# One pass of squares for two norms in a row: the sums of squares move to TensorE

## The chip, the cores and the metric

The kernel runs on one NeuronCore of a Trainium2 chip. The number that counts is the device time of one execution in microseconds (us), of which the median of the runs is taken.

## The reference, cut to what matters

The reference is a transformer block of width 1024 over 512 positions, then a second model of two layers whose input is the output of the first and 256 context rows. What is computed where the change lies:

```
x = x + gate2 * ((gelu(u_gate) * u_val) @ w_down)      # end of the first block
x = rmsnorm(x, g_final)                                # its final norm ("gfinal")
# second model, layer 0:
h = rms_norm(x, norm_g) * (1 + scale) + shift          # for the 512 latent rows, and the same for the 256 context rows
proj = h @ w_in                                        # first products: "pre"
rmsnorm(x, g) = x * rsqrt(mean(x*x) + 1e-6) * g
```

So two norms stand directly behind each other. All data are float32; the wide products split each operand into a rounded high part and a low part and add three products (high*high, low*high, high*low).

## The kernel before, in words

Activations are kept transposed: `XT` holds x as eight row groups of 128 channels by 512 positions, `CT` the context as eight of 128 by 256. The program is a list of stages (`plan()`), and each engine runs the stages in order from an instruction stream that is written out by hand. Counting semaphores `S[...]` order the engines, with a base count for each stage. Behind each stage stands a fence (line 3026): the engine drains, counts up, and in most stages waits for the other engines' counts. Nothing is scheduled automatically.

Around the change the stages are `up`, `down`, `gfinal`, `layer` (the norm of layer 0) and `pre`.

- `up` (PE line 2392, ACT 2656, DVE 2873) makes 22 groups F of the gated hidden layer. A group takes two 128x1024 weight blocks. ACT rounds a block into its high part (`act_high`, line 615), DVE makes its low part (`dve_low`, line 625), PE multiplies (`pe_split`, line 651), DVE does the convolution (lines 2890 to 2894), ACT the gelu (2665), DVE the gating product (`gated`, 2878). After the last group ACT rounds F rows 0 and 1 (2670) and DVE makes their low part (2911), which PE's first block of `down` needs. DVE then writes the modulation vectors (2693, 2698).
- `down` (PE 2411, ACT 2639, DVE 2919) has 22 weight blocks of 24 matmuls. Blocks with an even number add into PSUM banks 0 to 3 and those with an odd number into banks 4 to 7. Block 20 ends the first half and block 21 the second; DVE adds each half into `XT`, four times line 2941. ACT's DMA of the context rows into `SQ_ROWS` is issued in `down` (line 2035).
- `gfinal`: ACT squares each of the eight rows of `XT` (line 2092), DVE adds them up into one row `RS` (line 2055, one addition a row, each with a drain, three of them already between the halves of `down`), PE multiplies that row with ones, which gives the sum of each position (`pe_sums`, line 2072), ACT takes the root (2100), DVE the reciprocal (2143), PE spreads it over the partitions (`pe_spread`, 2062), and DVE scales `XT` in place, eight instructions (2150). Ahead of the sums PE transposes the context rows, 16 transposes (2021), which DVE copies into `CT` (2029).
- `layer` does the same again for the scaled `XT` and for `CT` together, 768 columns. Then DVE scales each row into a buffer (2150), ACT rounds it with the shift added (2110), DVE writes the low part (2160), and counts `low_row`. ACT and DVE first split the two first weight blocks of `pre` (615, 625).
- `pre` (PE 2433, ACT 2672, DVE 2947): PE's first two weight blocks go row by row behind `low_row` (`pe_rows_two`, line 655), then four more blocks j = 2 to 5. DVE copies each product out (2958) and splits the weights ahead. PE sums squares of the results in the same way as above (`pe_latent`, line 2203), without an addition ahead: the squares of three rows are multiplied with ones one after the other.

fp32 matmuls and sums appear in the trace as two instructions for each 128x128 tile (8 for four tiles), fp32 transposes as one.

## Time and profile before

| what | value |
|---|---|
| three runs | 3863.46, 3870.72, 3872.88 us |
| median | 3870.72 us |
| profiled execution, its own time | 3862.4 us |
| span inside it | 3860.6 us |
| TensorE (PE) busy | 3640.3 us, 94% |
| VectorE (DVE) busy | 2043.3 us, 53% |
| ScalarE (ACT) busy | 1426.3 us, 37% |
| mean granted TensorE clock | 0.975 of 2.4 GHz |

Times of the trace are counted from the start of the span. A row of the timeline view gives start, length, engine, line, operation and tiles, the number of merged instructions, and in brackets the idle time of that engine before it with what ended it. `<-DVE probs L2055` means that the wait ended when DVE's instruction on line 2055 did. `PEld` is TensorE's loading of the stationary operand.

### The profile page before, as it was taken

The numbers are of one execution on the slowest core, as the hardware profiler recorded it, in microseconds if no ns is written. First come the engines' busy times: TensorE is split into PE (matmuls) and PEld (weight loads), VectorE is DVE, ScalarE is ACT, GpSimd is POOL, SyncE is SP. The second block draws the span as 40 slices with busy tenths as digits, with TensorE's granted clock in tenths as the row PEclk, the third lists the DMA queues.
The fourth block names the chain that finished last, engine by engine and source line by source line (L and its number), as shares of the span: only waits on it lengthen the run. The fifth ranks groups of instructions, "written<-read, shape, count | busy, mean of one in ns | idle before, by whom it ended". The sixth has DMA issues, their size and how long they took to land.

```text
span 3860.6 us, 54876 instructions
## 1 busy us (share of the span) xinstructions
PE 3640.3 (94%) x20163; PEld 2824.5 (73%) x20163; DVE 2043.3 (53%) x3393; ACT 1426.3 (37%) x2534; POOL 265.7 (7%) x196
## 2 busy tenths in 40 slices
PE   6998989999799999999999999998999999999998
PEld 4665768878667788777778776886668777676666
DVE  4555346553545533777733555244553567645544
ACT  3433233323333322444431545122333344524532
POOL 0000000000011001111000100000110221001100
PEclk9998989999799999999999999997999999999999
DMA  7553325543101122211112111211113222131122
GB/s 257 158 138 95 92 85 165 167 139 109 50 21 30 27 65 58 52 48 50 44 49 57 42 28 50 66 55 49 29 37 93 61 64 55 49 92 51 42 77 79
DMA packets 506585, 286.93 MB, mean 74 GB/s; under 512 B 48129, under 2 KB 485469, under 8 KB 506438
## 3 DMA queue, kind: packets, MB, share of 16 engines
q1 hardware_dynamic: 485979, 264.60, 24.6%
q10 hardware_dynamic: 20459, 20.36, 1.8%
q8 instruction: 94, 1.54, 0.2%
q14 instruction: 53, 0.43, 0.0%
HBM read 269.05 MB, written 10.32 MB: 72 GB/s over the span
## 4 chain that ended last, share of the span: by engine, by line
issue 90%; PE 3%; POOL 3%; POOLq 2%; DVE 1%; ACT 0%; DVEq 0%; ACTq 0%
PE ps L629 3%; POOLq L1385 2%; POOL qT L1384 2%; POOL qT L1386 1%; POOL y_and_merged L1384 1%; DVEq L3028 0%; DVE w_low L625 0%; PE ps L2472 0%; DVE probs L911 0%; PE ps L1070 0%; POOLq L212 0%; DVE h_low L2270 0%; DVE y_low L2803 0%; ACT w_high L615 0%; DVE y_and_merged L3005 0%
## 5 line engine op out<-in xcount | busy, mean ns | idle before, releaser
L629 PE MATMUL ps<-h_high,w_high 128*128 128x512 f32 (+1 forms) x3432 | 1285.0, 374 | 45.9 <-DVE w_low L625 24.5
L629 PE MATMUL ps<-h_low,w_high 128*128 128x512 f32 (+1 forms) x3432 | 1246.7, 363 | 0.0
L629 PE MATMUL ps<-h_high,w_low 128*128 128x512 f32 (+1 forms) x3432 | 1243.7, 362 | 0.0
L629 PEld LDWEIGHTS ps<-h_high,w_high 128*128 128x128 f32 x3432 | 652.7, 190 | 209.5 <-issue 60.5
L625 DVE TENSOR_TENSOR w_low<-w_raw,w_high 128x1024 fp32r<-128x1024 f32 x374 | 463.3, 1239 | 590.2 <-ACT w_high L615 568.0
L629 PEld LDWEIGHTS ps<-h_high,w_low 128*128 128x128 f32 x3432 | 652.7, 190 | 103.3
L629 PEld LDWEIGHTS ps<-h_low,w_high 128*128 128x128 f32 x3432 | 654.0, 191 | 93.7 <-issue 3.1
L615 ACT ACTIVATE w_high<-w_raw 128x1024 fp32r<-128x1024 f32 x374 | 387.8, 1038 | 641.1 <-PE ps L629 549.4
L890 ACT ACTIVATE probs<-ps,neg_max 128x768 f32<-128x768 f32 (+1 forms) x240 | 194.8, 815 | 407.0 <-DVE neg_max L922 406.8
L629 PE MATMUL ps<-probsT,v 128*128 128x512 f32 (+4 forms) x736 | 285.7, 557 | 14.0 <-DVE probsT L1133 8.7
L922 DVE TENSOR_REDUCE neg_max<-ps 128x1 f32<-128x768 f32 (+1 forms) x240 | 196.7, 847 | 162.9 <-PE ps L629 152.9
L629 PE MATMUL ps<-y_high,w_high 128*128 128x512 f32 (+1 forms) x640 | 230.4, 360 | 8.1 <-issue 6.5
L629 PE MATMUL ps<-k_high,q_high 64*128 64x256 f32 (+4 forms) x784 | 181.5, 385 | 57.1 <-DVE neg_max L908 19.2
L629 PE MATMUL ps<-y_high,w_low 128*128 128x512 f32 (+1 forms) x640 | 229.8, 359 | 0.0
L890 ACT ACTIVATE probs<-probs,neg_max 128x512 f32<-128x512 f32 (+1 forms) x192 | 145.6, 758 | 172.0 <-DVE neg_max L914 123.1
L629 PE MATMUL ps<-y_low,w_high 128*128 128x512 f32 (+1 forms) x544 | 194.9, 358 | 0.0
L629 PEld LDWEIGHTS ps<-k_high,q_high 64*128 64x128 f32 (+1 forms) x784 | 88.9, 186 | 128.8 <-issue 31.5
L1019 PEld LDWEIGHTS ps<-ident,probs 128*128 128x128 f32 x832 | 101.6, 141 | 94.8 <-issue 85.3
L629 PE MATMUL ps<-k_low,q_high 64*128 64x256 f32 (+4 forms) x784 | 153.1, 323 | 0.0
L629 PE MATMUL ps<-k_high,q_low 64*128 64x256 f32 (+4 forms) x784 | 152.8, 322 | 0.0
L2807 DVE SCALAR_TENSOR_TENSOR probs<-probs,ps 128x512 f32<-128x512 f32 x88 | 51.9, 613 | 189.6 <-PE ps L629 189.6
L1133 DVE COPY probsT<-ps 128x512 f32<-128x512 f32 x112 | 73.2, 654 | 142.8 <-PE ps L1019 142.3
(250 smaller groups left out, 4158.6 us busy)
## 6 DMA issues: line engine op xcount, KB each, us to landing
w_raw<-in_w_in SPq DMA_DIRECT2D x436, 256.0 KB, 3.2
y_and_merged<-in_w_mod SPq DMA_DIRECT2D x96, 256.0 KB, 3.2
w_raw<-in_w_branch SPq DMA_DIRECT2D x96, 256.0 KB, 3.0
w_raw<-in_w_up SPq DMA_DIRECT2D x88, 256.0 KB, 4.3
y_and_merged<-in_w_ada SPq DMA_DIRECT2D x64, 256.0 KB, 3.2
w_raw<-in_w_out SPq DMA_DIRECT2D x48, 256.0 KB, 3.0
w_raw<-in_w_down SPq DMA_DIRECT2D x44, 256.0 KB, 3.2
y_and_merged<-in_w_ada SPq DMA_DIRECT2D x4, 2048.0 KB, 17.2
```

The costliest lines, as they stand in the source:

```text
L615: act.activation(WR[:, k, 0:nk], WRAW[:, k, 0:nk], ACT.Copy).then_inc(s_high, 1)
L625: nc.vector.tensor_tensor(WL[:, k, 0:nk], WRAW[:, k, 0:nk], WR[:, k, 0:nk].bitcast(F32), ALU.subtract).then_inc(s_low, 1)
L629: return nc.tensor.matmul(*a, **kw)
L890: act.activation(it["dst"], src, ACT.Exp, bias=NM[:, idx:idx + 1], accum_out=SL[:, idx:idx + 1]).then_inc(S["exped"], 1)
L922: v.tensor_reduce(NM[:, idx:idx + 1], src, AXX, ALU.max, negate=True).then_inc(S["maxed"], 1)
L1019: last = nc.tensor.transpose(PS[:, b:b + 128], tile, ident[:, :])
L1133: nc.vector.tensor_copy(PT[:, which, 0:m], PS[:, b:b + m]).then_inc(S["pt_dve"], 1)
L1384: g.tensor_tensor(x, x, cos, ALU.mult)
L1385: g.drain()
L1386: g.tensor_tensor(x, x, swapped, ALU.add).then_inc(S["roped"], 1)
L2807: v.scalar_tensor_tensor(out=d, in0=d, scalar=1.0, in1=p, op0=ALU.add, op1=ALU.mult)
```

## The change

The `layer` norm of layer 0 no longer has squares, sums, root and reciprocal of its own. In `gfinal` ACT squares the eight rows of `XT` once, into six buffers, and PE multiplies each square row as it comes with a pair of columns: ones, and g_final squared plus epsilon (`NORM_PAIR`). The second column gives the mean from which the root of both norms together follows: ACT takes it with a bias of epsilon squared (`EPS2`), and DVE's scaling in `layer` uses `GAINS`, the product of both gains, on the unscaled `XT`. The first column gives the final norm's own root `RX`, with which DVE scales `XT` itself later, two rows behind each of j = 1 to 4 of `pre`. The context rows' sums of squares come from two squaring instructions of ACT with an accumulated output, in block pair 3 of `down`. DVE's additions of squares (42 in the kernel before, line 2055) lose those of these two norms. PE transposes twelve context tiles ahead of the sums and four behind them; DVE copies all of them after the reciprocal. The two first weight splits of `pre` move to ahead of and in between the squares (ACT) and to behind the halves of `down` (DVE). PE no longer waits at the fence behind `down`, nor DVE at that behind `gfinal`. In `up`, the rounding of F rows 0 and 1 and their low part stand ahead of the last groups in place of behind them, and DVE's end of `up` gets five small instructions and two drains for the new columns.

```diff
+def shares_sums(s):
+    return s["what"] == "layer" and s["l"] == 0
...
         if k == "norm":
-            add(s, square=s["nk"], added=s["nk"] - 1, square_mm=1, rstd=1, rinv=1, spread=1)
+            if not shares_sums(s):
+                add(s, square=s["nk"], added=s["nk"] - 1, square_mm=1, rstd=1, rinv=1, spread=1)
             if s["what"] == "gfinal":
-                add(s, fin=8)
+                add(s, rstd=1, spread=1, fin=1)
...
+        NORM_PAIR = YM[:, 16 * TOK - 256:16 * TOK - 240].rearrange("p (k e) -> p k e", e=2)
+        GAINS = YM[:, 16 * TOK - 240:16 * TOK - 232]
+        EPS2 = YM[:, 16 * TOK - 232:16 * TOK - 231]
+        RX = YM[:, 16 * TOK - 228:16 * TOK - 224]
...
-            return [(x, 0, LAT, AC[:, 2 + 2 * l, kc:kc + 1], MOD[:, b, 0:1]),
+            return [(x, 0, LAT, GAINS[:, kc:kc + 1] if l == 0 else AC[:, 4, kc:kc + 1], MOD[:, b, 0:1]),
...
+        CT_BANKS = (1, 2, 3, 6)
+        def x_squares(kc):
+            return PP[:, 512 * (kc % 6):512 * (kc % 6) + 512]
+        def pe_both_norms(pe, s):
+            def turn(j):
+                for e in range(2):
+                    for a in range(2):
+                        kc = 2 * j + e
+                        last = nc.tensor.transpose(bank(CT_BANKS[j], 128, 256 * e + 128 * a), SQ_ROWS[:, a, 128 * kc:128 * kc + 128], ident[:, :])
+                last.then_inc(S["x_t"], 1)
...
+            pe.wait_ge(S["ctx_in"], s.base["ctx_in"] + 32)
+            pe.wait_ge(S["down_ev"], s.base["down_ev"] - 4)
+            for j in range(3):
+                turn(j)
+            for kc in range(NK):
+                pe.wait_ge(S["square"], s.base["square"] + kc + 1)
+                for tt in range(4):
+                    last = mm(bank(0, 2, 2 * tt), x_squares(kc)[:, 128 * tt:128 * tt + 128], NORM_PAIR[:, kc, :], start=kc == 0 and tt == 0,
+                              stop=kc == NK - 1, skip_group_check=True)
+                last.then_inc(S["added"] if kc < NK - 1 else S["square_mm"], 1)
+            turn(3)
+            pe.wait_ge(S["rinv"], s.base["rinv"] + 1)
+            pe_spread(4, RT, True).then_inc(S["spread"], 1)
+            pe.wait_ge(S["fin"], s.base["fin"] + 1)
+            pe_spread(7, RX, False).then_inc(S["spread"], 1)
+        def act_both_norms(act, s):
+            first = Stage("first", h_end=None).at(s.base)
+            act_high(act, first, 0, 0, 0)
+            for kc in range(NK):
+                if kc == 4:
+                    act_high(act, first, 0, 0, 1)
+                act.wait_ge(S["down_ev"], s.base["down_ev"] - 8 + kc + 1)
+                if kc >= 6:
+                    act.wait_ge(S["added"], s.base["added"] + kc - 5)
+                act.activation(x_squares(kc), XT[:, kc, :], ACT.Square).then_inc(S["square"], 1)
+            act.drain()
+            act.activation(RT[:, 4:6], RT[:, 4:6], ACT.Sqrt, scale=1.0 / D, bias=EPSB[:, :])
+            act.wait_ge(S["square_mm"], s.base["square_mm"] + 1)
+            sums = bank(0, 8).rearrange("p (a e) -> p a e", e=2)
+            act.activation(RT[:, 0:4], sums[:, :, 1], ACT.Sqrt, scale=1.0 / D, bias=EPS2).then_inc(S["rstd"], 1)
+            act.activation(RX, sums[:, :, 0], ACT.Sqrt, scale=1.0 / D, bias=EPSB[:, :]).then_inc(S["rstd"], 1)
+        def dve_both_norms(dve, s):
+            def rows(j):
+                dve.wait_ge(S["x_t"], s.base["x_t"] + 8 + j + 1)
+                nc.vector.tensor_copy(CT[:, 2 * j:2 * j + 2, :], bank(CT_BANKS[j]).rearrange("p (e t) -> p e t", e=2))
+            dve_low(dve, Stage("first", h_end=None).at(s.base), 0, 0, 1)
+            dve.wait_ge(S["rstd"], s.base["rstd"] + 1)
+            nc.vector.reciprocal(RT[:, 0:6], RT[:, 0:6]).then_inc(S["rinv"], 1)
+            rows(0)
+            rows(1)
+            dve.wait_ge(S["rstd"], s.base["rstd"] + 2)
+            nc.vector.reciprocal(RX, RX)
+            rows(2)
+            rows(3)
+            nc.vector.drain().then_inc(S["fin"], 1)
+        def dve_scaled_x(s, rows):
+            for kc in rows:
+                nc.vector.scalar_tensor_tensor(out=XT[:, kc, :], in0=XT[:, kc, :], scalar=VT[:, V_GFIN + kc:V_GFIN + kc + 1], in1=bank(7),
+                                               op0=ALU.mult, op1=ALU.mult)
         def pe_norm(pe, s):
-            if s["what"] == "h1":
+            if s["what"] == "h1" or shares_sums(s):
                 return
-            if s["rows"]:
-                pe_rows(pe, s)
...
             pe_sums(pe, s)
...
+            if s["what"] == "gfinal":
+                act_both_norms(act, s)
+                return
+            if shares_sums(s):
+                for kc in range(nk):
+                    act_rounded(act, s, kc)
+                return
...
-                if s["what"] == "gfinal":
-                    act.wait_ge(S["down_ev"], s.base["down_ev"] - 8 + kc + 1)
-                if s["what"] == "layer" and s["l"] == 0:
-                    act.wait_ge(S["fin"], s.base["fin"] - 8 + kc + 1)
                 act_row(act, s, kc)
...
-            if s["what"] == "gfinal":
-                last.then_inc(S["fin"], 1)
...
-            if s["what"] == "layer" and s["l"] == 0:
-                for j in range(2):
-                    dve_low(dve, Stage("first", h_end=None).at(s.base), 0, 0, j)
-            for kc in range(6 if done_in_out(s) else 4 if s["rows"] else 1, NK):
+            if s["what"] == "gfinal":
+                dve_both_norms(dve, s)
+                return
+            if shares_sums(s):
+                dve.wait_ge(S["spread"], s.base["spread"] - 1)
+                for kc in range(NK):
+                    dve_scaled(dve, s, kc)
+                    if kc:
+                        dve_low_row(dve, s, kc - 1)
+                dve_low_row(dve, s, NK - 1)
+                return
+            for kc in range(6 if done_in_out(s) else 1, NK):
                 dve_add(dve, s, kc, s["ctx"])
-            if s["rows"]:
-                dve_rows(dve, s, (0, 1))
...
             dve_inverse(dve, s)
-            if s["rows"]:
-                dve_rows(dve, s, (2, 3))
...
+                    if kb == 3:
+                        act.wait_ge(S["ctx_in"], stages[s.index + 1].base["ctx_in"] + 32)
+                        for a in range(2):
+                            act.activation(PP[:, D * a:D * a + D], SQ_ROWS[:, a, :], ACT.Square, accum_out=RT[:, 4 + a:5 + a])
+                        act.drain()
                     for e in range(2):
                         act_high(act, s, 0, 0, 2 * kb + 2 + e)
...
                 repeat(act, NF - 2, 2, body)
-                for u in range(2):
-                    body(NF // 2 - 1, u, NF - 2 + u)
                 for a in range(2):
                     last = act.activation(f_rows(0, a)[0], F[:, a, :], ACT.Copy)
                 last.then_inc(S["f_high"], 1)
+                for u in range(2):
+                    body(NF // 2 - 1, u, NF - 2 + u)
...
                 with dve.Fori(1, NF // 2 - 1) as t:
                     for u in range(2):
                         body(t, u, t * 2 + u)
-                for u in range(2):
-                    body(NF // 2 - 1, u, NF - 2 + u)
-                gated(NF // 2 - 1, 1, NF - 1)
+                body(NF // 2 - 1, 0, NF - 2)
                 dve.wait_ge(S["f_high"], s.base["f_high"] + 1)
                 for a in range(2):
                     fh, fl = f_rows(0, a)
                     last = v.tensor_tensor(fl, F[:, a, :], fh.bitcast(F32), ALU.subtract)
                 last.then_inc(S["f_low"], 1)
+                body(NF // 2 - 1, 1, NF - 1)
+                gated(NF // 2 - 1, 1, NF - 1)
                 dve.wait_ge(S["mod_sum"], s.base["mod_sum"] + 44)
                 modulation(v, 52, 96, bank(7, 88), V_BMOD + 4)
                 v.drain()
                 for a, (m0, c, g) in enumerate(((56, 0, V_NG), (56, 1, V_NG), (80, 0, V_NG + 8), (80, 1, V_NG + 8))):
                     norm_scale(v, a + 2, m0, c, g)
+                gain = VT[:, V_GFIN:V_GFIN + 8]
+                v.memset(NORM_PAIR[:, :, 0], 1.0)
+                v.memset(EPS2, EPS * EPS)
+                v.tensor_tensor(NORM_PAIR[:, :, 1], gain, gain, ALU.mult)
+                v.drain()
+                v.tensor_scalar(NORM_PAIR[:, :, 1], NORM_PAIR[:, :, 1], EPS, None, ALU.add)
+                v.tensor_tensor(GAINS, AC[:, 2, :], gain, ALU.mult)
+                v.drain()
...
                     if hf == 0:
-                        v.drain()
-                        for kc in range(1, 4):
-                            dve_add(dve, s, kc, False)
+                        dve_low(dve, Stage("first", h_end=None).at(stages[s.index + 1].base), 0, 0, 0)
...
                     last.then_inc(S["mm_ev"], 1)
+                    if l == 0 and 1 <= j <= 4:
+                        if j == 1:
+                            dve.wait_ge(S["spread"], s.base["spread"])
+                        dve_scaled_x(s, (2 * j - 2, 2 * j - 1))
...
                 return
-            if me == "act" and (s.kind == "down" or s["what"] == "gfinal"):
+            if me in ("act", "pe") and s.kind == "down" or s["what"] == "gfinal":
                 return
-            if me == "pe" and (s["what"] == "gfinal" or s.kind == "up"):
+            if me == "pe" and s.kind == "up":
                 return
             for other in s_fence:
```

## Rows read from the trace of the kernel before

The columns of the timeline are start us, length us, engine, line, operation, out<-in, shapes and count, [idle before <- what ended it]. The columns of the stretches are length, busy us of PE, PEld, DVE, ACT and POOL (each with its count), granted clock, share of the DMA engines, GB/s.

**Rows 1.** First part of the page: busy time of each engine.

```profile
PE 3640.3 (94%) x20163; PEld 2824.5 (73%) x20163; DVE 2043.3 (53%) x3393; ACT 1426.3 (37%) x2534; POOL 265.7 (7%) x196
```

**Rows 2.** Waits of PE: engine, tile, line, releaser: total us, times, longest.

```profile
PE ps L629 <- DVE probs L2055: 27.8, 4, 15.2
```

**Rows 3.** Timeline of PE around the two norms, 978 to 1013 us.

```profile
978.01 0.39 PE L629 MATMUL ps<-h_high,w_low 128*128 128x512 f32 x1
981.31 3.32 PE L2021 MATMUL ps<-ident,probs 128*128 128x128 f32 x16 [2.91 <-DVEq L3028]
...
986.12 1.16 PE L629 MATMUL ps<-ident,rstd_rows 128*128 128x128 f32 x8 [0.57 <-DVE rstd_rows L2143]
1002.50 2.72 PE L629 MATMUL ps<-ones,probs 128*128 128x2 f32 x12 [15.22 <-DVE probs L2055]
1005.80 2.93 PE L629 MATMUL ps<-ident,rstd_rows 128*128 128x128 f32 x12 [0.58 <-DVE rstd_rows L2143]
1012.38 0.77 PE L629 MATMUL ps<-h_high,w_high 128*128 128x512 f32 x1 [3.66 <-DVE h_low L2160]
```

**Rows 4.** Timeline of DVE, same stretch.

```profile
978.43 2.73 DVE L2941 SCALAR_TENSOR_TENSOR xT<-ps,mod,xT 128x512 f32<-128x512 f32 x4 [0.28 <-PE ps L629]
...
984.54 1.29 DVE L2029 COPY y_and_merged<-ps 128x512 f32<-128x512 f32 x2
...
987.32 5.35 DVE L2150 SCALAR_TENSOR_TENSOR xT<-xT,vectors,ps 128x512 f32<-128x512 f32 x8
...
995.19 7.25 DVE L2055 TENSOR_TENSOR probs<-probs 128x768 f32<-128x768 f32 x7
...
1008.76 0.75 DVE L2150 SCALAR_TENSOR_TENSOR probs<-xT,norm_scale,ps 128x512 f32<-128x512 f32 x1 [3.02 <-PE ps L629]
```

**Rows 5.** Timeline of ACT, same stretch.

```profile
973.86 1.95 ACT L2092 ACTIVATE probs<-xT 128x512 f32<-128x512 f32 x3 [5.19 <-DVE xT L2941]
...
986.02 2.00 ACT L615 ACTIVATE w_high<-w_raw 128x1024 fp32r<-128x1024 f32 x2 [0.17 <-issue]
...
1005.25 0.27 ACT L2100 ACTIVATE rstd_rows<-ps,eps 128x6 f32<-128x6 f32 x1 [3.94 <-PE ps L629]
```

**Rows 6.** PE's thin work at the full clock, elsewhere (timeline).

```profile
1049.18 4.73 PE L629 MATMUL ps<-ones,probs 128*128 128x2 f32 x36
...
2534.64 1.96 PE L2021 MATMUL ps<-ident,probs 128*128 128x128 f32 x16
```

**Rows 7.** Busy time by stretch; the number behind POOL is the granted clock.

```profile
983.00:984.00 1.00, 1.00 (x7) 1.00 (x6) 0.91 (x2) 0.55 (x1) 0.00 (x0) 0.50 0.02 8
984.50:986.00 1.50, 1.05 (x10) 0.97 (x8) 1.40 (x4) 0.26 (x1) 0.00 (x0) 1.00 0.00 0
...
1051.00:1052.00 1.00, 1.00 (x11) 1.00 (x11) 0.00 (x0) 0.28 (x1) 0.00 (x0) 1.00 0.00 0
...
1053.00:1054.00 1.00, 1.00 (x6) 1.00 (x6) 0.00 (x0) 0.05 (x1) 0.00 (x0) 0.50 0.00 0
```

**Rows 8.** Edge from `up` to `down`: PE (timeline, then clock), DVE, ACT.

```profile
855.91 0.76 PE L629 MATMUL ps<-q_high,w_high 128*128 128x512 f32 x1 [4.34 <-DVE k_low L2911]
...
855.90:861.00 5.10, 5.09 (x12) 4.04 (x13) 2.83 (x7) 2.00 (x2) 0.00 (x0) 0.50 0.17 50
...
846.05 1.23 DVE L625 TENSOR_TENSOR w_low<-w_raw,w_high 128x1024 fp32r<-128x1024 f32 x1 [3.98 <-ACT w_high L615]
...
852.03 0.75 DVE L2894 SCALAR_TENSOR_TENSOR probs<-ps,vectors,probs 128x511 f32<-128x511 f32 x1
...
831.43 1.06 ACT L615 ACTIVATE w_high<-w_raw 128x1024 fp32r<-128x1024 f32 x1 [1.33 <-DMA w_raw<-in_w_up]
...
856.56 1.06 ACT L615 ACTIVATE w_high<-w_raw 128x1024 fp32r<-128x1024 f32 x1 [2.08 <-DVEq L3028]
```

**Rows 9.** Cover in `down` (ACT) and in `pre` (DVE), timeline.

```profile
962.17 1.06 ACT L615 ACTIVATE w_high<-w_raw 128x1024 fp32r<-128x1024 f32 x1 [3.43 <-PE ps L629]
...
1074.60 1.02 DVE L2958 COPY qT<-ps 96x512 f32<-96x512 f32 x2 [3.76 <-PE ps L629]
```

11 lines of the change are left out of this document (6 added, 5 removed).

## The prediction

> **What bounds the kernel now.** I read the page first: TensorE is busy 94% of the span, no other engine over 53% [rows 1]. So a gain must come from places where TensorE stands still or runs at half clock. Next the list of PE's waits: its largest is the one for DVE's additions of squares on line 2055, 27.8 us in four waits, one of them 15.2 us long [rows 2]. Then PE's timeline where that long wait lies. The last matmul of `down` starts at 978.01 and ends at 978.40; the first matmul of `pre` starts at 1012.38 [rows 3]. Between them PE only has 16 transposes, two small sums and two spreadings. **34.0 us** pass in which the chain over DVE and ACT sets the time: DVE brings x up to date until 981.16, adds, scales XT in place for 5.35 us, adds again for 7.25 us over 768 columns, and scales from 1008.76 [rows 4]. From that first scaling to the first matmul of `pre` it is 1012.38 - 1008.76 = 3.62 us [rows 3, 4]. Last I read the granted clock of the same stretch and of others with thin matmuls [rows 7], and the edge from `up` to `down`, which the change also touches [rows 8].
>
> **The change, part by part: between the norms.** Out of the path go the second set of squares and additions, the second root, reciprocal and spreading, and the 5.35 us of scaling XT. What is new on the path is PE's: 8 rows by 4 tiles by 2 = 64 instructions in place of 8 and 12.
>
> The start: PE no longer waits 2.91 us for the fence [rows 3]. Its twelve transposes need the context and the first half's banks, both there. They begin at about 978.45. Such a transpose took 1.96/16 = 0.123 us at the full clock [rows 6], so 1.5 us, until 979.95. Squares are ready by then: ACT splits the first weight block from about 973.1 (1.00 us each by rows 5), then squares rows 0 to 3 at 0.65 us each [rows 5] until 976.8. It takes the second block at 978.43 and rows 4 to 7 from 979.45; the last cannot begin ahead of DVE's last update, 981.16 [rows 4], and is done by about 983 with its wait for a free buffer. PE needs it only after seven rows of sums, so ACT is never last. DVE's splits (two, one in the half break and one behind 981.16) also lie ahead of what comes.
>
> The sums: 4.73/36 = 0.131 us each at the full clock [rows 6], 2.72/12 = 0.227 us at half [rows 3]. 64 cost 8.4 us or 14.5 us. Which clock? In the row with 36 such sums in one piece the clock was 1.00 at 1051 and 0.50 at 1053 [rows 7], although PE had no gap: dense thin sums did not keep the clock, and it fell some 3.3 us into them. I take the same here: it falls 3.4 us after 978.45, at 981.85. By then (981.85 - 979.95)/0.131 = 14 sums are done; 50 x 0.227 = 11.3 us follow, so the sums end at 993.2. Bounds: full clock throughout, 988.4; half clock from the first transpose, 978.45 + 12 x 0.207 [3.32/16, rows 3] + 14.5 = 995.5.
>
> Behind the sums: from their end to the first spreading it was 1005.80 - 1005.22 = 0.58 us for root and reciprocal [rows 3, 5]. Four transposes stand ahead of the spreading now, 0.83 us at half clock, so it starts 0.83 behind the sums; twelve instructions of 2.93 us [rows 3], and DVE starts 0.03 later: 3.8 us. Beside it DVE makes the reciprocal, four copies at 0.65 us [rows 4], a second reciprocal and a drain: about 0.5 + 2.6 + 0.2 + 0.2 = 3.5 us, hidden (at full clock PE needs 0.58 + 1.16 x 12/8 = 2.3 us and DVE's 3.5 us become the path). Then 3.62 us as before. First matmul of `pre`: 993.2 + 3.8 + 3.6 = 1000.6, against 1012.38: **11.8 us saved**. The bounds: 995.5 + 7.4 = 1002.9, which saves 9.4; 988.4 + 3.5 + 3.6 = 995.5, which saves 16.9. The second spreading of PE (eight, 1.16 us [rows 3] to 1.95 us) waits for DVE's `fin` and falls into the 3.66 us in which PE waits for the first `low_row` [rows 3]. I cost it at nothing; without that cover it is 2 us.
>
> Here a page speaks against the change. The clock at 983 was 0.50 and at 984.5 it was 1.00 [rows 7], with nothing but transposes in between [rows 3]. The Trainium skill, TensorE: Matmul & The Clock Gate, section Part 4: PE-mode transpose, says that transposes do not count as TensorE being busy. This trace disagrees for these fp32 transposes. By the page the twelve new ones would help the clock fall and the sum would go to its slow bound, 9.4 us; by the row they hold it for a while.
>
> **In `pre`.** XT's eight scalings, 5.35 us [rows 4], are now two behind each of four products, 1.34 us at a time. DVE waits for PE there: ahead of the last copy it still stood idle for 3.76 us [rows 9], the shortest of the stretches these fall in. Cost nothing; uncovered they would be 5.4 us. In `down` ACT gets two squares of 1024 columns, about 1.1 us each with the accumulator (estimate from its 1.06 us for 1024 columns [rows 9]), into an idle piece of 3.43 us [rows 9]. Nothing; without the cover 2.2 us. The weights' DMAs on SP's queue wait for DVE's splits, which come sooner than before.
>
> **The edge from `up` to `down`.** PE waited 4.34 us for the low part of F row 1 and began at 855.91 [rows 8]. Both roundings now stand ahead of ACT's split at 831.43, where it waited 1.33 us for a DMA, and cost about 1.2 us; both low parts stand ahead of DVE's at 846.05, with 3.98 us idle and a cost of 1.3 us [rows 8]. Hidden. What is late next is the last convolution, 852.03 + 0.75 = 852.78, for which PE waits too. So PE starts at 852.88, 3.0 us sooner. The new small instructions (about 0.8 us, an estimate: root and reciprocal of six columns took 0.58 together [rows 3], hand-overs included, for two of them) lie behind DVE's gating product, which moved up by as much as the low parts took (1.3 us). ACT's next split was at 856.56, behind DVE's fence [rows 8], and comes at about 856, so block 1 can start at 858.3, when block 0 (24 matmuls of 0.227, 5.45 us) ends. And the clock: before, the first twelve matmuls ran at 0.50 [rows 8], 0.427 in place of 0.227 us, which cost 2.4 us. With 1.3 us of idle in place of 4.3 the clock may hold or fall later. Bounds 0 and 2.4 us, less 0.2 for the wait of block 1; I take 1.4, a little over the middle, since the idle time is so much shorter. **4.4 us saved**, bounds 3.0 and 5.2.
>
> **The sum.** 11.8 + 4.4 = 16.2 us. Against the profiled execution's own time that is 3862.4 - 16.2 = 3846.2. That execution stood 8.3 us under the median of the runs shown (3870.72), within their spread of 9.4 us; on the scale of the median it is **3854.5 us**.
>
> **The rivals.**
> First, the clock holds: full speed through sums and edge, 16.9 + 5.2 = 22.1 us, 3848.6 us. For it, the clock stood at 1.00 in the sums of the first norm [rows 7]; against it the 36 sums behind which it was 0.50 [rows 7].
> Second, half clock from the first transpose and no clock gain at the edge, 9.4 + 3.0 = 12.4 us, 3858.3 us. This is what the page's rule would make of the norms. For it, PE is cold by 983 today [rows 7]; against it, that was after 2.91 us of idle, which goes.
> Third, given back behind the norms: the clock falls more often in the stages behind. The place is where PE's work is broken by waits. Price 2.4 us for each fall (twelve matmuls at 0.427 for 0.227, rows 8). From 16.2/2.4 = seven more falls than before the kernel is slower; ten would give 3862.4 + 24 - 16.2, that is 3878.5 us on the median's scale. For it: the three runs differ by 9.4 us with the same program. Against it: PE is busy 94% [rows 1], and nothing behind `pre` is changed.
> That the change doesn't do what it says: the long wait stays because ACT or DVE is late for PE's sums. Against it are the times above, seven rows of sums ahead of the last square. Then the gain would be that of the edge alone, 3867 us.
>
> **How the numbers follow.** Forecast 0.60, clock holds 0.15, half clock 0.15, given back 0.07 (half of it slower), not as it says 0.03. The range 3844 to 3862 takes in the first three cases with 4 us for the runs' scatter, and leaves out most of the last two. What a measurement of this kernel can tell from no change is about 0.3%, 11.6 us, so faster means under 3859.1: all of the forecast but its slow edge, all of the first rival, over half of the second: 0.55 + 0.15 + 0.08 = 0.78. Slower 0.04, the rest 0.18.
>
> **What would show it.** In PE's timeline: twelve transposes directly behind the last matmul of `down`, 64 sums of 0.13 and then 0.23 us, and some 22 us instead of 34.0 to the first matmul of `pre`; the granted clock falling within the sums; the wait for line 2055 at about 12 us in total instead of 27.8. At the edge a wait of about 1.3 us for DVE's line of the last convolution. In `pre` DVE still idle ahead of each copy. The prediction is wrong if the sums take 0.23 us from the first or 0.13 to the last, if PE waits for ACT's squares, or if the stages behind `pre` change their length.

## The result, and the profile after

| | kernel before | changed kernel |
|---|---|---|
| median, us | 3863.18 (6 runs, 3855.36 to 3872.88) | 3840.76 (6 runs, 3833.3 to 3849.04) |
| profiled execution: own time / span, us | 3862.4 / 3860.6 | 3840.41 / 3838.6 |

The ratio is 0.9941, 95% interval 0.993 to 0.9952: the change saves 22.4 us, nearly twice the 0.3% that a measurement of this kernel can tell from nothing. The forecast was 3854.5 in a range of 3844 to 3862. The sign and the mechanism were right; the time lies 3 us below the range. One of the runs of the kernel before that stood beside the experiments took 5931 us at a mean granted clock of 0.556 and is left out everywhere.

The page of the changed kernel, first part. TensorE's busy share is 95% instead of 94% and its busy time 4.4 us longer [rows 1]: PE took over work, and its gaps shrank.

```profile
PE 3644.7 (95%) x20207; PEld 2830.1 (74%) x20207; DVE 2029.5 (53%) x3384; ACT 1420.6 (37%) x2523; POOL 265.9 (7%) x196
```

Waits of PE in the changed kernel. The line of [rows 2] (now 2064) has 12.9 us where it had 27.8; its longest wait, 15.2 us, is gone.

```profile
PE ps L639 <- DVE probs L2064: 12.9, 4, 5.2
```

Timeline of PE in the changed kernel around the norms; the last product of `down` starts at 969.85. This answers to [rows 3].

```profile
969.85 0.39 PE L639 MATMUL ps<-h_high,w_low 128*128 128x512 f32 x1
970.50 1.50 PE L2100 MATMUL ps<-ident,probs 128*128 128x128 f32 x12 [0.26 <-issue]
971.84 10.89 PE L639 MATMUL ps<-y_and_merged,probs 128*128 128x2 f32 x64
982.59 1.09 PE L2100 MATMUL ps<-ident,probs 128*128 128x128 f32 x4
983.47 2.77 PE L639 MATMUL ps<-ident,rstd_rows 128*128 128x128 f32 x12
986.03 1.91 PE L639 MATMUL ps<-ident,y_and_merged 128*128 128x128 f32 x8
989.90 0.47 PE L639 MATMUL ps<-h_high,w_high 128*128 128x512 f32 x1 [1.95 <-DVE h_low L2247]
```

From the end of the last product of `down`, 970.24, to the first product of `pre` it is 19.7 us, where it was 34.0. No wait is left inside but 0.26 us ahead of the transposes and 1.95 us ahead of `pre`. The granted clock in the sums (columns as in [rows 7]): 0.72 in the stretch from 974 to 976 is full speed for 0.88 us of two, so it fell at about 974.9, 3.0 us after the first sum. By the start times of the single instructions in the trace, the sums follow each other at 0.112 us before that and at 0.213 us behind it; 28 of them start before the fall. The first row belongs to the edge from `up` to `down`, further below.

```profile
850.25:860.00 9.75, 9.75 (x43) 8.07 (x44) 5.27 (x14) 3.68 (x4) 0.00 (x0) 1.00 0.21 67
...
974.00:976.00 2.00, 2.00 (x16) 2.00 (x15) 0.47 (x1) 0.71 (x2) 0.00 (x0) 0.72 0.09 18
976.00:978.00 2.00, 2.00 (x11) 2.00 (x11) 0.00 (x0) 0.00 (x0) 0.00 (x0) 0.50 0.82 244
...
984.00:986.00 2.00, 2.00 (x11) 2.00 (x11) 1.67 (x4) 0.00 (x0) 0.00 (x0) 0.50 0.00 0
```

DVE's timeline in the changed kernel: between the last update of x and the first scaling it has only small work, and stands idle for 8.59 us while PE sums. The two rows from `pre` show its copy and, behind it, two of the eight scalings that stood on the path before [rows 4].

```profile
970.28 2.73 DVE L3047 SCALAR_TENSOR_TENSOR xT<-ps,mod,xT 128x512 f32<-128x512 f32 x4 [1.50 <-PE ps L639]
...
983.06 0.19 DVE L2152 RECIPROCAL rstd_rows<-rstd_rows 128x6 f32<-128x6 f32 x1 [8.59 <-ACT rstd_rows L2139]
...
986.28 0.75 DVE L2239 SCALAR_TENSOR_TENSOR probs<-xT,y_and_merged,ps 128x512 f32<-128x512 f32 x1 [0.61 <-PE ps L639]
...
1018.55 1.02 DVE L3062 COPY y_and_merged<-ps 128x512 f32<-128x512 f32 x2 [4.87 <-PE ps L639]
1019.49 1.40 DVE L2165 SCALAR_TENSOR_TENSOR xT<-xT,vectors,ps 128x512 f32<-128x512 f32 x2
...
1052.13 1.02 DVE L3062 COPY qT<-ps 96x512 f32<-96x512 f32 x2 [2.85 <-PE ps L639]
```

The edge from `up` to `down` in the changed kernel (PE's timeline). Instead of 4.34 us PE waits 1.20, for the last convolution, and `down` runs at clock 1.00 at once (the row from 850.25 above, in which PE has no gap) where it ran at 0.50 [rows 8].

```profile
848.67 0.38 PE L639 MATMUL ps<-pick,mod_buffers 128*128 128x2 f32 x2 [0.40 <-ACT mod_buffers L721]
850.25 0.50 PE L639 MATMUL ps<-q_high,w_high 128*128 128x512 f32 x1 [1.20 <-DVE probs L2992]
```

To compare whole executions I cut each trace at the same instructions. **Ahead** is all until the last product of the modulation's sum (848.67 above). **B** goes from there to DVE's first update of x in `down`: the edge and the first half of `down`. **C** goes on to the first product of `pre`: the second half and the norms. **D** is `pre` until the copy of its last product (1052.13 above), and **behind** is the rest until the first copy of the output; its instructions are the same in all kernels. The last 8 to 9 us of the span, behind that copy, stand in no column.

| us | ahead | B | C | D | behind | span |
|---|---|---|---|---|---|---|
| kernel before | 851.2 | 121.9 | 39.3 | 62.2 | 2777.1 | 3860.6 |
| changed kernel | 848.7 | 116.2 | 25.0 | 62.2 | 2777.9 | 3838.6 |
| difference | -2.5 | -5.7 | -14.3 | 0.0 | +0.8 | -22.0 |

So 20.0 us come from the two places that the change touches (B and C). The stretch ahead has the same instructions in both; it came out between 848.1 and 851.2 over all traces below, so its 2.5 us are scatter.

### The profile page after: what moved, and what is told of

It reads as the page before. It is cut to its first block, busy times and chain, and to the rows that moved or that the text cites. A ratio compares the mean times of both kernels' runs of the same rounds, so it can differ in the third digit from the quotient of the medians.

```text
span 3838.6 us, 54925 instructions
## 1 busy us (share of the span) xinstructions
PE 3644.7 (95%) x20207; PEld 2830.1 (74%) x20207; DVE 2029.5 (53%) x3384; ACT 1420.6 (37%) x2523; POOL 265.9 (7%) x196
## 4 chain that ended last, share of the span: by engine, by line
issue 90%; PE 3%; POOL 3%; POOLq 2%; DVE 1%; ACT 0%; DVEq 0%; ACTq 0%
PE ps L639 3%; POOLq L1395 2%; POOL qT L1394 2%; POOL qT L1396 1%; POOL y_and_merged L1394 1%; DVEq L3137 0%; DVE w_low L635 0%; DVE probs L921 0%; PE ps L1080 0%; POOLq L218 0%; DVE h_low L2362 0%; DVE y_and_merged L3114 0%; PE ps L2564 0%; DVE y_low L2901 0%; ACT w_high L625 0%
```

## Experiments

Line numbers in rows of experiments are those of their own text. Times are medians, ratios are to the kernel before on the same chip with their 95% interval; cuts are those of the table above. The theory that they test: the gain is 14.3 us of the norms, sized by PE's sums and their clock, plus 5.7 us of the edge, partly waiting and partly clock. The rivals: the gain comes from something else (the fence that PE no longer waits for, the eight scalings that left the path), or from the stages behind.

**The two halves of the change alone.** The first kernel is the changed one with the old order at the end of `up`; the second is the kernel before with the new order there.

```
e1_old_edge (against the changed kernel; the same exchange in ACT's and DVE's part)
-                for a in range(2):
-                    last = act.activation(f_rows(0, a)[0], F[:, a, :], ACT.Copy)
-                last.then_inc(S["f_high"], 1)
                 for u in range(2):
                     body(NF // 2 - 1, u, NF - 2 + u)
+                for a in range(2):
+                    last = act.activation(f_rows(0, a)[0], F[:, a, :], ACT.Copy)
+                last.then_inc(S["f_high"], 1)
e2_edge_only (against the kernel before): the same lines with - and + exchanged
```

> The changed kernel with the old order at the end of up: the rounding of F rows 0 and 1 and their low part stand behind the last groups again. Theory (the two parts of the gain are independent and add; the edge is worth 3.1 us of waiting and 2.4 us of half clock): 5.5 us slower than the changed kernel, 14 to 17 us faster than the kernel before; PE's first block of down starts behind a wait of over 4 us again. Rival (the edge's gain is only clock luck of one execution): within 2 us of the changed kernel, and no wait of over 4 us. In the trace from the end of down to the first product of pre: 19.7 us as in the changed kernel by both.

> The kernel before with only the new order at the end of up. Theory: 5.5 us faster than the kernel before (3.1 of waiting, 2.4 of clock), ratio about 0.9986, and 34.0 us from the end of down to the first product of pre. Rival (the end of down waits for something else, so that the edge is given back): ratio 1.000.

The old edge in the changed kernel took 3838.96 us, 0.9933 (0.9919 to 0.9947). The new edge alone took 3857.26 us, 0.9984 (0.9975 to 0.9993). In PE's timelines the waits are the ones named in the prediction, 4.21 us for the low part and 1.08 us for the last convolution:

```profile
855.57 0.76 PE L556 MATMUL ps<-q_high,w_high 128*128 128x512 f32 x1 [4.21 <-DVE k_low L2510]
...
979.62 9.93 PE L556 MATMUL ps<-y_and_merged,probs 128*128 128x2 f32 x64
```

```profile
852.32 0.50 PE L548 MATMUL ps<-q_high,w_high 128*128 128x512 f32 x1 [1.08 <-DVE probs L2419]
...
997.21 2.72 PE L548 MATMUL ps<-ones,probs 128*128 128x2 f32 x12 [15.22 <-DVE probs L1723]
```

The new edge alone is worth 5.8 us in stretch B (121.9 to 116.1) and 5.8 us in the median. The norms alone shorten C to 24.0. (With the new edge alone, C is 0.8 us longer than in the kernel before, 40.1, and D 1.6 us shorter, 60.6.) But the halves don't add up: 5.8 and 24.1 us by medians, 22.4 together. The changed kernel is no faster than the one with the old edge, against the 5.5 us expected. Both kernels were therefore run a second time, on one chip.

> The changed kernel once more, unaltered, on the same chip as the run with the old order at the end of up. Both theories expect a ratio to the kernel before of 0.993 to 0.9955. What it is for: the difference to the next run. If the edge's 5.5 us count in whole, this one is 4 to 7 us faster than the next; if they are given back behind it, less than 2 us. Theory for the scatter between executions: the code ahead of the change and the stages behind it differ by some us from one execution to the next although they are the same instructions; in the trace the last product of up's modulation (851.18 us before, 848.67 us after) and the way from pre to the end should again move by up to 3 us each.

> The changed kernel with the old order at the end of up, once more. In its first run the trace showed the edge as before (wait of 4.21 us) and from it to the second half of down 121.7 us against 116.2 in the changed kernel, but the median was 3839.0 against 3840.8 us of the changed kernel. Theory (the edge counts, the first medians differ by chance): 3 to 7 us slower than the changed kernel on this chip. Rival (given back: without the wait at the edge, the clock falls more often or DVE and ACT are later in the stages behind): within 2 us of it.

The changed kernel came to 3836.85 (0.9939, 0.9926 to 0.9951), the one with the old edge to 3838.01 (0.9943, 0.993 to 0.9956). All 11 runs of the changed kernel have a mean of 3838.97, all 10 with the old edge 3839.06. By stretches, each with its two traces:

| us | ahead | B | C | D | behind |
|---|---|---|---|---|---|
| changed | 848.7, 849.5 | 116.2, 116.1 | 25.0, 25.1 | 62.2, 62.2 | 2777.9, 2769.3 |
| old edge | 851.0, 848.1 | 121.7, 121.8 | 24.0, 23.9 | 60.6, 60.7 | 2771.2, 2772.4 |

The 5.6 us of B are there both times. 2.7 of them are given back both times. C is 1.1 us longer, since the clock falls after 28 sums instead of 38 (64 sums in 10.89 us against 9.93). And `pre` is 1.6 us longer, since the half clock behind the start of its own 36 sums lasts twice as long: from 1029.5 to 1036.3 in the changed kernel, from 1038.3 to 1041.7 with the old edge. First the changed kernel's rows, then those with the old edge; 36 sums at full clock take 4.08 us.

```profile
1026.69 5.12 PE L639 MATMUL ps<-ones,probs 128*128 128x2 f32 x36
...
1029.60:1036.20 6.60, 6.60 (x22) 5.63 (x22) 1.29 (x2) 0.27 (x1) 0.00 (x0) 0.50 0.27 63
1037.00:1052.00 15.00, 15.00 (x96) 12.74 (x94) 6.71 (x11) 1.84 (x2) 0.00 (x0) 1.00 0.00 1
```

```profile
1033.52 4.08 PE L556 MATMUL ps<-ones,probs 128*128 128x2 f32 x36
...
1001.00:1038.00 37.00, 36.17 (x219) 31.30 (x217) 21.70 (x37) 12.46 (x18) 0.00 (x0) 1.00 0.23 58
1038.50:1041.50 3.00, 3.00 (x8) 2.32 (x7) 0.72 (x1) 0.00 (x0) 0.00 (x0) 0.50 0.38 89
1042.00:1057.00 15.00, 15.00 (x96) 12.84 (x95) 6.71 (x11) 1.84 (x2) 0.00 (x0) 1.00 0.03 7
```

The other 3 us are less than what the stretches ahead and behind differ by between two executions of one kernel, and can't be placed. Most of that scatter is itself the clock. The two executions of the changed kernel, in one stretch of the second layer's attention between the same two POOL instructions, with the same 98 matmuls, 19 instructions of DVE and 19 of ACT (first the run of the result, then the second; columns as in [rows 7]):

```profile
2671.40:2693.80 22.40, 20.51 (x98) 15.12 (x97) 10.82 (x19) 10.74 (x19) 3.75 (x4) 0.92 0.18 46
```

```profile
2668.50:2689.20 20.70, 18.90 (x98) 14.55 (x97) 10.84 (x19) 10.76 (x19) 3.77 (x4) 1.00 0.20 49
```

With the clock at 0.92 in the mean (one fall to 0.50 in it) the stretch takes 22.4 us, at 1.00 it takes 20.7. Over the whole stretch behind, the trace's records of the granted clock put 90.3 us at 0.50 in the first execution and 75.1 us in the second; half of the difference, 7.6 us, is an estimate of what the clock cost, and the stretch differs by 8.6 us. The same division was made for a second trace of the kernel before.

> The kernel before once more, for a second trace of it. Theory (what moves between executions of one kernel lies in the stages that the change leaves alone; the stretches at the change repeat): from the last product of up's modulation to the first update of x 121.9 us, from there to the first product of pre 39.3 us, from that to the copy of the last product of pre 62.2 us, each within 0.3 us or moved by the clock by 1 to 2 us; the stages behind (2777.1 us from there to the first copy of the output) different by 3 to 8 us. Rival (the stretches at the change move too by several us): those three differ by over 3 us in sum.

It took 3864.26 us in one run, with 849.2, 121.7, 39.3, 62.2 and 2781.3 in its stretches: B, C and D are those of the first trace to 0.2 us, and the stretch behind is 4.2 us longer. Over the three traces with the old norms the stretch behind took 2777.1, 2778.3 and 2781.3, over the eleven with changed norms 2773.6 in the mean, with a standard deviation of 3.0. So the stages behind `pre` came out 5.3 us shorter with the changed norms, though their instructions are the same. The totals say so too: 42 runs of the kernel before, those beside all the experiments included, have a mean of 3863.5 us, 24.5 more than the 11 of the changed kernel and the 10 with the old edge, while the stretches B, C and D account for 20.0 and for 17.1 us. The half clock in that stretch lasts 85 us in the mean of the three traces and 78 us in that of the eleven, which makes some 4 of the 5.3 us, an estimate as above. Why the clock falls less often there is not shown, and three traces on one side are few.

**The fence.** PE waits for DVE's fence at the end of `down` again.

```
e3_pe_fence (against the changed kernel)
-            if me in ("act", "pe") and s.kind == "down" or s["what"] == "gfinal":
+            if me == "act" and s.kind == "down" or s["what"] == "gfinal":
```

> The changed kernel, in which PE waits again at the fence behind down for ACT and DVE. Theory: PE's twelve transposes start some 2.7 us later, behind DVE's last update of x, and everything behind them too; the clock falls nearer to their start, so more sums run at half clock: 2.7 to 5 us slower than the changed kernel. Rival (DVE or ACT bound the stretch, not PE): no change.

3839.9 us, 0.9942 (0.9927 to 0.9956). PE's timeline has the wait of [rows 3], and the sums behind it:

```profile
974.52 1.50 PE L1754 MATMUL ps<-ident,probs 128*128 128x128 f32 x12 [2.91 <-DVEq L2616]
975.86 10.26 PE L556 MATMUL ps<-y_and_merged,probs 128*128 128x2 f32 x64
...
993.30 0.77 PE L556 MATMUL ps<-h_high,w_high 128*128 128x512 f32 x1 [2.62 <-DVE h_low L1868]
```

The wait starts the transposes 2.65 us later (2.91 for 0.26). 2.0 us of it arrive in C (27.0); the sums are 0.6 us shorter than in the changed kernel, since the clock fell 3.7 us after the first of them. `pre` then took 60.6 us, so the total shows nothing of it, against the 2.7 to 5 us expected. The fence is a term of 2 us and no rival for the 14.3.

**The price of a sum.** Every sum is issued twice; the second result goes to columns that nobody reads.

```
e4_double_sums (against the changed kernel)
                 for tt in range(4):
+                    mm(bank(0, 2, 64 + 2 * tt), x_squares(kc)[:, 128 * tt:128 * tt + 128], NORM_PAIR[:, kc, :], start=False,
+                       stop=kc == NK - 1, skip_group_check=True)
                     last = mm(bank(0, 2, 2 * tt), ...
```

> The changed kernel with each of the 32 two-column products of squares made twice (the second result goes unused): 64 more instructions of PE. Theory (PE sets the time of this stretch, and thin products at half clock take 0.227 us): 14.5 us slower, nearly all at 0.227 us, since the clock falls about as late as before; the stretch from the end of down to the first product of pre grows from 19.7 to about 34 us. Rival 1 (PE at full clock once it is kept busy): 8.4 us slower. Rival 2 (ACT's squares bound it): 5 us or less.

3854.41 us, 0.9976 (0.9965 to 0.9988). PE's timeline, and a stretch within the sums:

```profile
974.97 23.30 PE L556 MATMUL ps<-y_and_merged,probs 128*128 128x2 f32 x128
...
1005.45 0.47 PE L556 MATMUL ps<-h_high,w_high 128*128 128x512 f32 x1 [2.00 <-DVE h_low L1870]
```

```profile
985.00:990.00 5.00, 5.00 (x25) 5.00 (x25) 0.00 (x0) 0.00 (x0) 0.00 (x0) 0.50 0.02 3
```

128 sums in a row without a gap, and the clock stays at 0.50: it fell at about 979.4 and does not come back before their end. The sums start 0.213 us apart there (the 25 of the row above count those that stand over its ends), not 0.227 as in the forecast. The 64 more made C 12.4 us longer (37.4). 41 sums ran before the fall instead of 28, so the 64 more are 13 at 0.112 and 51 at 0.213, 12.3 us: the path from `down` to `pre` is bound by PE's sums, one to one. Its B is 118.1: there the clock did fall at the edge. Over the ten traces with the new edge B is 116.1 or 116.2 in seven, with waits of 1.08 to 1.20 us at the edge, and 117.9 to 118.1 in three (this one, the two dense products, the scalings on the path), with waits of 1.26 to 1.40 us. The instructions are the same, so 2 us of the edge hang on the clock. The total is 15.4 us over the mean of the changed kernel; its trace places 12.4 in C and 2.0 in B.

**Can wide products keep the clock?** One, then two products of 512 columns stand among every eight sums (behind the sixth); their results are not used. In the first row PE also waits until DVE has read the bank that they write.

```
e5_one_dense (e6_two_dense: range(2))
+                if kc == 0:
+                    pe.wait_ge(S["down_ev"], s.base["down_ev"] - 3)
+                for e in range(1):
+                    mm(bank(4), HR[:, 0, 0:128], HR[:, 1, 0:512], start=True, stop=True, skip_group_check=True)
```

> The changed kernel with one dense product of 128x512 (result unused) among the four thin ones of each of the eight rows, eight products of 0.23 us. Theory (thin products alone let the clock fall; dense ones count): too few dense columns (0.23 of each 1.3 us), the clock still falls; the stretch grows by 1.8 to 3.2 us. Rival (any dense work in between keeps the clock): the sums take 8.4 + 1.8 = 10.2 us in place of 10.9 and the spreadings, at full clock, 1 us less: up to 2 us faster.

> The changed kernel with two dense products of 128x512 among the four thin ones of each row of squares (results unused), where one left the clock falling 3.3 us behind the first sum. Theory: with 0.46 us of dense work in each 1.5 us the clock may be kept; then the sums take 8.4 + 3.5 = 11.9 us and the spreadings are at full clock (1.7 and 1.2 us). Rival (it falls all the same): 15 us for the sums, 0.50 in the clock from some 4 us behind the first.

One: 3838.01 us, 0.9945 (0.9931 to 0.9959). Two: 3846.97 in one run. The clock fell in both, here in PE's timeline with one dense product: the same eight sums take 0.95 us and then 1.70.

```profile
974.25 0.95 PE L556 MATMUL ps<-y_and_merged,probs 128*128 128x2 f32 x8
975.05 0.61 PE L556 MATMUL ps<-h_high 128*128 128x512 f32 x1
975.46 1.70 PE L556 MATMUL ps<-y_and_merged,probs 128*128 128x2 f32 x8
```

C became 28.0 and 30.2: the added products cost 3.0 and 5.2 us and save only what the spreadings behind them gain from the clock's return (2.27 and 1.16 us for 2.77 and 1.91 with one). This much padding is no way to hold the clock here; more of it was not tried.

**The sums the other way round.** The two columns (ones and squared scales) become the stationary operand, and the squares of a row stream through as 512 columns: eight products (16 instructions) in place of 32 (64 instructions). Root and reciprocal then work on 2 rows of 512, and PE spreads each root with one product. The context's last transposes, its copies and its own spreading move ahead of the last sum. In the second kernel PE turns the two rows of roots back into columns first (four small products with the identity), so that DVE's reciprocals are 128 by 4 again.

```
e7_squares_move (against the changed kernel)
-                for tt in range(4):
-                    last = mm(bank(0, 2, 2 * tt), x_squares(kc)[:, 128 * tt:128 * tt + 128], NORM_PAIR[:, kc, :], ...
+                last = mm(bank(0)[0:2, :], NORM_PAIR[:, kc, :], x_squares(kc), start=kc == 0, stop=kc == NK - 1, ...
...
+            nc.vector.reciprocal(RR, RR).then_inc(S["rinv"], 1)      # RR: 2 x 512
e12_turned_back (against e7_squares_move)
+            for tt in range(4):
+                last = mm(bank(7, 2, 2 * tt), RR[:, 128 * tt:128 * tt + 128], ident[0:2, 0:2], ...
-            nc.vector.reciprocal(RR, RR).then_inc(S["rinv"], 1)
+            nc.vector.reciprocal(RT[:, 0:4], both[:, :, 1]).then_inc(S["rinv"], 1)      # 128 x 4
+            nc.vector.reciprocal(RX, both[:, :, 0])
```

> The changed kernel with the operands of the sums exchanged: the pair of columns (ones, squared gains plus epsilon) is loaded and the 512 columns of squares stream through, eight fp32 products of 2x512 in place of 64 thin instructions. ACT takes both roots from one 2x512 row pair, DVE one reciprocal of it, and PE spreads each with one product of 128x512; the context's two roots, their spreading and all copies of context rows lie ahead of the last sum. Theory (the sums are 1.0 us a row at best because of 128x128 loads, and streaming 512 columns counts as activity for the clock): an fp32 product of 512 columns is four times the 0.216 us of a rounded one, 0.87 us a row, 7.0 us in all, the clock stays at 1.00; root and reciprocal of 512 columns about 0.6 us each, spreading 0.9: from the end of down to the first product of pre 1.8 + 7.0 + 0.5 + 1.3 + 0.9 + 3.6 = 15 us in place of 19.7, so 4 to 5 us faster than the changed kernel, whose spread of medians is as large. Rival (two loaded columns leave the array nearly empty and the clock falls all the same): 1.7 us a row at half clock, 22 us and more.

> As the run in which the squares stream through (2x512 sums, 6.2 + 1.0 us there at full clock), but without its reciprocal of 2x512, which took 3.34 us, in which PE waited 4.14 us and behind which the clock fell. Here ACT takes the root of the 2x512 row pair (0.68), PE turns it back into 128x2 a tile (eight thin instructions, 1.0 us), DVE takes the reciprocals of 128x4 (0.2 each), PE spreads with eight instructions (1.2 us at full clock). Theory: first scaling 5.4 us behind ... in numbers, sums end 9.9 us behind the last product of down, plus 0.8 + 1.1 + 0.3 + 1.2 = 3.4 us, plus 3.6 us: 17.0 us from the end of down to the first product of pre, against 19.7 in the changed kernel and 18.9 with the long reciprocal; 2.7 us in the total, less than its medians can tell. Rival (the hand-overs eat it, or the clock falls before the spreading): 18.5 us or more.

The first took 3837.69 us, 0.9943 (0.993 to 0.9956). PE's timeline, DVE's reciprocal, and the clock in the sums:

```profile
972.01 6.17 PE L556 MATMUL ps<-probs,y_and_merged 128*2 128x512 f32 x14
...
984.31 2.97 PE L556 MATMUL ps<-probsT,ident 2*128 2x512 f32 x4 [4.14 <-DVE probsT L1797]
989.24 0.77 PE L556 MATMUL ps<-h_high,w_high 128*128 128x512 f32 x1 [1.96 <-DVE h_low L1865]
```

```profile
980.92 3.34 DVE L1797 RECIPROCAL probsT<-probsT 2x512 f32<-2x512 f32 x1 [1.42 <-ACT probsT L1786]
```

```profile
972.00:978.00 6.00, 6.00 (x15) 1.11 (x14) 4.26 (x7) 2.37 (x5) 0.00 (x0) 1.00 0.32 89
```

Seven products (14 instructions) take 6.17 us at the full clock, and it holds; with the eighth (1.02 us) the sums cost 7.19 us where they cost 10.89. The reciprocal of 2 by 512 eats that: 3.34 us, where 128 by 4 takes 0.17 to 0.19. PE waits 4.14 us for it, the clock falls after all, and C is 24.2. The second kernel took 3839.47 us, 0.994 (0.9926 to 0.9953):

```profile
982.20 1.05 PE L556 MATMUL ps<-ident,probsT 2*128 2x2 f32 x8 [0.77 <-ACT probsT L1791]
983.52 1.16 PE L556 MATMUL ps<-ident,rstd_rows 128*128 128x128 f32 x8 [0.28 <-DVE rstd_rows L1803]
984.51 1.06 PE L556 MATMUL ps<-ident,y_and_merged 128*128 128x128 f32 x8
988.33 0.47 PE L556 MATMUL ps<-h_high,w_high 128*128 128x512 f32 x1 [2.76 <-DVE h_low L1873]
```

```profile
983.28 0.18 DVE L1803 RECIPROCAL rstd_rows<-ps 128x4 f32<-128x4 f32 x1 [2.52 <-PE ps L556]
```

Here the spreadings take 1.16 and 1.06 us, the clock holds to the end, and C is 22.1 us, the shortest of all: 2.9 less than in the changed kernel. A part of that is the context's work that moved ahead of the last sum; no run separates it. The median does not show the gain; 3 us are no more than its uncertainty. It is the better form of this piece by its trace, and not measurably a faster kernel.

**The scalings back on the path.** DVE scales x in place, eight times, ahead of the layer norm's scaling. The layer norm thus reads x scaled twice (its factors are those of the unscaled x), and its results are not the reference's; the scalings are the same eight instructions as in the kernel before, and the time alone counts.

```
e11_scale_in_path (against the changed kernel)
-                    if l == 0 and 1 <= j <= 4:      (in `pre`, with its wait and its two scalings)
...
-                dve.wait_ge(S["spread"], s.base["spread"] - 1)
+                dve.wait_ge(S["spread"], s.base["spread"])
+                dve_scaled_x(s, range(NK))
+                nc.vector.drain()
```

> The changed kernel with DVE's eight scalings of x by the final norm put back ahead of the layer norm's scaling in place of in pre. (The layer norm then reads x scaled twice; its time alone is of interest.) Theory (DVE is the path there and has cover in pre): the first product of pre comes 5.4 us later for the scalings and 1.7 for the second spreading, for which they wait, 7 us together; pre itself stays as long as before, so 5 to 8 us slower than the changed kernel. Rival (in pre the scalings cost as much as they save): within 2 us.

3843.13 us, 0.9948 (0.9934 to 0.9962), 4.2 us over the mean of the changed kernel. DVE's timeline, then PE's:

```profile
987.76 5.36 DVE L1803 SCALAR_TENSOR_TENSOR xT<-xT,vectors,ps 128x512 f32<-128x512 f32 x8 [2.32 <-PE ps L556]
```

```profile
973.03 9.46 PE L556 MATMUL ps<-y_and_merged,probs 128*128 128x2 f32 x64
...
996.81 0.77 PE L556 MATMUL ps<-h_high,w_high 128*128 128x512 f32 x1 [9.09 <-DVE h_low L1868]
```

PE's wait ahead of `pre` grows from 1.95 to 9.09 us, 7.1 us: 5.4 of scalings, the rest the later spreading that they need. C grows by only 5.7 (30.7), since the sums had 1.4 us less (9.46; the clock fell 4.6 us after the first). And D is 59.0, 3.2 us below the changed kernel's. The clock accounts for all of that: here it stays at 1.00 in `pre` until the copy of its last product.

```profile
1002.00:1056.00 54.00, 53.28 (x321) 46.03 (x320) 23.98 (x41) 14.03 (x19) 0.00 (x0) 1.00 0.19 50
```

D took 62.2 us with the longer stretch at half clock behind the start of `pre`'s own sums (eight traces), 60.6 with the shorter one (five traces), and 59.0 here with none: 1.6 us at each step. The kernel before, without any scaling in `pre`, took 62.2 as well, and with the new edge alone 60.6. So the scalings cost nothing in `pre`, and moving them off the path is worth 5.4 us, as the forecast has it (5.7 in C here).

**What stays untested.** By these runs 2.0 of the 14.3 us of the norms are the fence and 5.7 the scalings. The other 6.6, about, belong to the one pass of squares and to the move of the sums from DVE to PE together; no run has one without the other.

## Why the prediction was wrong

**The base** is the step that put the time outside the range. The gain was taken off the profiled execution, 3862.4 us, which gave 3846.2; then 8.3 us were added to come to the median of three runs, 3870.72. Three more runs put that median at 3863.18. The error of 13.7 us is made of 7.5 for this step, 2.5 for the norms, 1.3 for the edge and 2.4 that the total has beyond the two places. With the six runs' median as the base the forecast would have been 3847.0, and the time within a range of the same width. The profiled execution would have been a better base here by luck: it too is one draw, 0.8 us under the median in the kernel before, 0.35 in the changed one, and 6.0 in the one with double sums.

**The sums** were mis-sized. Forecast: 14.8 us from the end of `down` to the end of the sums [rows 3, 6]. Measured: 982.73 - 970.24 = 12.5. Both prices were averages with something else in them. The 0.131 us for full clock came from 36 sums of 4.73 us [rows 6], in which the clock had already fallen, as the row at 1053 shows [rows 7]; 36 sums at full clock throughout take 4.08 us, and single ones start 0.112 us apart. The 0.227 us at half clock came from twelve instructions whose first latency was in the average [rows 3]; they start 0.213 us apart. And the clock was to fall 3.4 us after the first transpose, with 14 sums done; it fell 4.4 us after it, 3.0 us into the sums, with 28 done. 14 at 0.131 and 50 at 0.227 are 13.2 us, 28 at 0.112 and 36 at 0.213 are 10.8: the later fall is 1.4 us of the difference (14 x 0.101), the prices are 1.0 us. The other terms held: transposes 1.50 us for 1.5; from the sums to the first product of `pre` 7.2 us for 7.4. The norms saved 14.3 us instead of 11.8, within the bounds of 9.4 and 16.9.

**The edge** was sized at 4.4 us and gave 5.7. The waiting was 3.1 us for 3.0. The clock gave 2.5 us where I took 1.4: it held at 1.00. The 0.2 us for a wait of block 1 did not come. So 5.7 lies a little above the upper bound of 5.2, and as the traces with B at 118 show, it is one of two outcomes. Inside the changed kernel this 5.7 is worth less than by itself, since the clock then falls earlier in the sums and stays at half longer in `pre`: 2.7 us back, in both pairs of traces. In the kernel before, the same edit made C 0.8 us longer and D 1.6 us shorter, so its sign is not fixed. The third rival named this (falls behind the change at 2.4 us each), as a loss from seven falls on; here it is one fall earlier and one longer, at 1.1 and 1.6.

**The covers** held. D is 62.2 us before and after. DVE stands idle for 4.87, 4.87, 9.03 and 2.85 us ahead of the copies that follow the pairs of scalings, against 5.96, 5.96, 9.40 and 3.76 in the kernel before. ACT was never last: its squares ended at 974.41, and PE's last row of sums began at 980.9. ACT's wait ahead of its split at the end of `up` shrank from 1.33 to 0.44 us with the roundings in it.

**The rivals.** The clock did not hold in the sums (0.50 from 976 on). It was not at half from the first transpose either: twelve transposes ran in 1.50 us, 0.125 each, at the full clock, and the clock fell some 3 us after they had ended. By the Trainium skill, TensorE: Matmul & The Clock Gate, section Part 4: PE-mode transpose, a transpose does not count as TensorE being busy in the same way. The new row doesn't settle that, since a fall 4.4 us after the first transpose fits either reading; against that sentence still stands the rise of the clock behind nothing but transposes [rows 3, 7], and the slow case of the forecast did not come. The prediction's last sign of being wrong, stages behind `pre` of another length, did not show in the two traces of the result (0.8 us) and does over all traces (5.3 us shorter, see above).

**What the total adds.** 20.0 us are located (5.7 + 14.3); the profiled spans differ by 22.0 and the medians by 22.4. The 2 us more are the stretch ahead (2.5) less the stretch behind (0.8), both with unchanged instructions. The interval of the ratio, about 18.5 to 27 us, holds 20.0 and does not exclude the 24.5 by the means of all runs.

## What to carry to other kernels

A chain DVE, ACT, PE with waits in between can be worth rewriting as more work on the engine that is otherwise full: with 44 more instructions on PE the path is 14.3 us shorter, because PE stood idle there. Of that, 2.0 us are a fence that PE no longer waits for and 5.7 us work of DVE that moved off the path. Price such instructions by the distance of their starts in a stretch whose clock does not change, not by the length of a row with a clock fall or a first latency in it. A median of three runs that scatter by 9.4 us is no sure base for a forecast of 16.2 us; its uncertainty belongs into the range. Where the clock matters, a sum can be made by streaming wide operands past a narrow stationary one; here that shortened the piece by its trace and not measurably the kernel. Keep the reciprocal on 128 partitions and few columns.

## What the hardware showed that I had not expected

- Dense two-column products do not keep the clock, with no gap for 23.30 us; it fell 3.0 us (result), 3.7 (fence), 4.1 (old edge), 4.4 (double sums) and 4.6 us (scalings on the path) after the first of them. Streaming 512 columns past two stationary ones kept it at 1.00 for 6.17 us.
- DVE's reciprocal goes by columns and not by partitions: 3.34 us for 2 by 512 and 3.35 us in the mean for the 16 of 128 by 512 later in the changed kernel, 1.69 us for 128 by 256, 0.17 to 0.19 for 128 by 4 and 128 by 6.
- A gain ahead moves later clock falls, either way: in two pairs of traces of kernels that differ only at the end of `up`, the norms 120 us later took 1.1 us more and `pre` 1.6 us more; with the norms of the kernel before, the same difference made 0.8 us more and 1.6 us less.
- Two executions of one kernel differ by the clock in stretches of unchanged work: 22.4 us at a mean of 0.92 against 20.7 us at 1.00 in one of them, and 90.3 against 75.1 us at half clock over the whole stretch behind `pre`.
